# First mixer: twelve sums of squares per layer as two rounded products

## The chip, the cores and the metric

The kernel runs on one core of a Trainium2 chip. The metric is the device time of one execution in microseconds. Five engines work side by side, each with its own queue of instructions in order: TensorE (PE in the profile; its weight loads, PEld, overlap its products), VectorE (DVE), ScalarE (ACT), GpSimd (POOL) and SyncE (SP, which here only starts transfers). They wait for each other by semaphores.

## The reference, cut to what matters

Two stacks of two layers each work on 256 rows of 1024 features. A layer of the first stack is feed-forward, mixer, feed-forward. The change lies in the mixer of the first stack, where the queries and keys of both branches are normalised for each head of 128 features:

```python
def l2norm(x):
    xf = x.astype(jnp.float32)
    return xf * lax.rsqrt(jnp.sum(xf * xf, axis=-1, keepdims=True) + L2_EPS)

def hybrid_mixer(h, w_in, conv_w, ...):
    dn_qkv, dn_z, dn_b, dn_a, sb_q, sb_k, sb_v, gate_a, gate_b = split_cols(h @ w_in)
    qkv = jax.nn.silu(causal_depthwise_conv(dn_qkv, conv_w))
    q, k, v = jnp.split(qkv, 3, axis=-1)
    q = l2norm(to_heads(q, DN_HEADS, DN_HEAD_DIM))
    k = l2norm(to_heads(k, DN_HEADS, DN_HEAD_DIM))
    ...
    o_a = gated_delta_rule_chunked(q, k, v, g, beta)
    ...
    qb = rmsnorm(to_heads(sb_q, SB_HEADS, SB_HEAD_DIM), sb_q_norm)
    kb = rmsnorm(to_heads(sb_k, SB_HEADS, SB_HEAD_DIM), sb_k_norm)
    o_b = stick_breaking_attention(qb, kb, vb)
```

Each of the four (q, k of one branch, sq, sk of the other) has eight heads. Two heads are handled together, so there are sixteen sums of squares in a layer, numbered 0 to 15 here in the order in which they are made.

## The kernel before

The big products are made from weights and inputs that are split in two: a rounded part (`whi`, `xhi`, type float32r) and the rest (`wlo`, `xlo`), and three products of these parts stand for one (`product3`, lines 275 to 277). A weight unit is 128x2048 numbers in one of three slots. For each unit SyncE loads it (`load_unit`, line 246), ScalarE rounds it (`split_hi`, 252), VectorE forms the rest (`split_lo`, 267), and TensorE multiplies.

The first mixer (`mix1_pe`, `mix1_act`, `mix1_dve`, `mix1_pool`, one function for each engine) runs a loop over 28 units of two heads, in the order of the table `IN1`: sk0, sq0, q0, sv0, sk1, q1, sq1, sv1, and so on. The order of work on each engine is what these functions write out; nothing reorders it. `NORM` is the list of the sixteen units that have a norm, `SILU` that of the units which go through a silu, `CONV` that of the units with a convolution. What is done for unit n is spread over the turns of the loop:

- turn n: TensorE multiplies unit n; ScalarE copies it out of its bank (`keep_unit_act`, 880 to 884); VectorE does the convolution (1040, 1044).
- turn n+1: the silu: ScalarE's Abs, Exp, Ln (852 to 856), VectorE's minimum (866), ScalarE's last Exp (861) at the end of its turn, GpSimd's product (`silu_pool`, 871).
- turn n+2: ScalarE squares it into `sqr`, one of two buffers (921).
- turn n+3: TensorE, behind the products of unit n+3, multiplies the squares with a 128x128 matrix of ones (779): the sum over the 128 features, in every row of a bank. It is a product of plain fp32 numbers.
- turn n+4: ScalarE's Ln and Exp of the sum (928, 933); turn n+5: VectorE's scaling (1006, 1008).

Behind the sum, TensorE has in some turns the small products of the stick-breaking attention (1158 to 1182), one head after another, with ScalarE's Abs, Exp, Ln and weights (1199 to 1210), VectorE's parts (1192, 1219, 1224) and the copies of the result to `yhi` and `ylo` (1214, 1228). After the loop comes the delta rule (`mix1_delta_*`).

`yhi` and `ylo` hold the stick-breaking result, head g in column g, and are otherwise free in this loop.

## Time and profile before

| | |
|---|---|
| time, median of 3 runs | 2453.53 us (2451.59 to 2453.79) |
| span of the profiled execution, first to last instruction | 2447.8 us |
| TensorE busy | 2402.2 us, 98% |
| VectorE busy | 1537.0 us, 63% |
| ScalarE busy | 1380.4 us, 56% |
| GpSimd busy | 143.5 us, 6% |
| granted TensorE clock, mean | 0.994 |
| fp32 sums of squares (line 779) | 32 products of 128x512, 64 records |

The span is shorter than the time of an execution by what lies before its first and behind its last instruction; the time of the profiled execution itself is not listed apart from the three runs. The records of TensorE's products are pipelined: a 128x256 product has a record of 0.28 us, but the next one starts 0.12 us after it, so times are read from start to start. Records of the other engines overlap a little too. An fp32 product shows as two records. The loop of the mixer that is changed runs from about 213 to 415 us in layer 0, and from about 988 to 1190 us in layer 1.

### The profile page before, as it was taken

Reading aid. Unit: us, or ns where it says so; the run is one execution under the profiler, and the core shown is the slowest. Engines: PE = TensorE matmul, PEld = TensorE weight load, DVE = VectorE, ACT = ScalarE, POOL = GpSimd, SP = SyncE. Lnnn points to the kernel's source line nnn. Section 1 sums busy time; section 2 is a strip of 40 time slices with the busy share of each in tenths; the row PEclk is TensorE's granted clock in tenths of the full one; section 3 lists DMA queues with packets and bytes.
Section 4 is the critical chain, followed back from the end, with each engine's and each line's share of the span. In section 5 each row is a group of like instructions: output and inputs, shape, how many; then the busy total and the mean of one; then the engine's idle time right before and its main releaser. Section 6 shows DMA issues by size and latency. Waiting matters only on the chain.

```text
span 2447.8 us, 40865 instructions
## 1 busy us (share of the span) xinstructions
PE 2402.2 (98%) x17253; PEld 2238.3 (91%) x17253; DVE 1537.0 (63%) x1867; ACT 1380.4 (56%) x1854; POOL 143.5 (6%) x117
## 2 busy tenths in 40 slices
PE   7999999999999999999999999999999999999998
PEld 7998999998998999899999899888989989888998
DVE  5555678746555655667865655568585455958545
ACT  5455788265555554678635554546654454665444
POOL 0000013000000000001300000000030000004000
PEclk9999999999999999999999999999999999999999
DMA  6554443234554555444314555544445654435553
GB/s 227 194 183 150 160 138 121 87 104 157 201 182 166 190 189 181 148 144 134 119 53 161 175 181 190 191 127 122 137 163 186 200 189 137 130 121 175 192 191 121
DMA packets 312310, 386.58 MB, mean 158 GB/s; under 512 B 10796, under 2 KB 287296, under 8 KB 312128
## 3 DMA queue, kind: packets, MB, share of 16 engines
q1 hardware_dynamic: 311848, 383.87, 47.6%
q8 instruction: 137, 2.24, 0.4%
q14 instruction: 45, 0.37, 0.0%
q10 hardware_dynamic: 280, 0.10, 0.0%
HBM read 382.89 MB, written 1.06 MB: 157 GB/s over the span
## 4 chain that ended last, share of the span: by engine, by line
PE 87%; DVE 7%; ACT 4%; issue 2%; DMA 0%; SPq 0%; DVEq 0%; ACTq 0%
PE bank L275 26%; PE bank L276 25%; PE bank L277 25%; DVE arena L1044 2%; DVE wlo L267 2%; PE bank L1306 1%; PE bank L1311 1%; PE bank L779 1%; ACT whi L252 1%; PE bank L1317 1%; PE bank L1891 1%; PE bank L1283 1%; DVE x L325 1%; DVE arena L2179 1%; ACT arena L356 0%
## 5 line engine op out<-in xcount | busy, mean ns | idle before, releaser
L275 PE MATMUL bank<-xhi,whi 128*128 128x256 f32 x3712 | 1065.9, 287 | 5.6 <-ACT xhi L383 3.5
L276 PE MATMUL bank<-xlo,whi 128*128 128x256 f32 x3712 | 1053.3, 284 | 0.0
L277 PE MATMUL bank<-xhi,wlo 128*128 128x256 f32 x3712 | 1053.3, 284 | 0.0
L267 DVE TENSOR_TENSOR wlo<-raw,whi 128x2048 fp32r<-128x2048 f32 x360 | 831.2, 2312 | 337.8 <-ACT whi L252 334.2
L252 ACT ACTIVATE whi<-raw 128x2048 fp32r<-128x2048 f32 x351 | 669.1, 1907 | 231.4 <-PE bank L277 229.1
L275 PEld LDWEIGHTS bank<-xhi,whi 128*128 128x128 f32 x3712 | 715.1, 193 | 15.3 <-issue 8.3
L276 PEld LDWEIGHTS bank<-xlo,whi 128*128 128x128 f32 x3712 | 715.3, 193 | 4.7 <-issue 1.9
L277 PEld LDWEIGHTS bank<-xhi,wlo 128*128 128x128 f32 x3712 | 714.8, 193 | 0.0
L275 PE MATMUL bank<-whi,yhi 128*128 128x512 f32 x608 | 237.5, 391 | 0.0
L276 PE MATMUL bank<-wlo,yhi 128*128 128x512 f32 x608 | 237.4, 390 | 0.0
L277 PE MATMUL bank<-whi,ylo 128*128 128x512 f32 x608 | 236.5, 389 | 0.0
L277 PEld LDWEIGHTS bank<-whi,ylo 128*128 128x128 f32 x608 | 114.1, 188 | 24.1
L275 PEld LDWEIGHTS bank<-whi,yhi 128*128 128x128 f32 x608 | 114.5, 188 | 22.0
L276 PEld LDWEIGHTS bank<-wlo,yhi 128*128 128x128 f32 x608 | 114.4, 188 | 21.2
L2318 DVE TENSOR_SCALAR arena<-bank 128x512 f32<-128x512 f32 x32 | 22.1, 692 | 148.5 <-PE bank L277 148.5
L606 DVE SCALAR_TENSOR_TENSOR arena<-bank,arena 128x512 f32<-128x512 f32 x44 | 30.4, 692 | 134.4 <-ACT arena L533 134.4
L529 ACT ACTIVATE arena<-bank 128x512 f32<-128x512 f32 x44 | 26.3, 597 | 149.6 <-PE bank L277 149.6
L275 PE MATMUL bank<-yhi,whi 128*128 128x256 f32 x384 | 108.8, 283 | 0.0
L277 PE MATMUL bank<-yhi,wlo 128*128 128x256 f32 x384 | 108.7, 283 | 0.0
L276 PE MATMUL bank<-ylo,whi 128*128 128x256 f32 x384 | 108.7, 283 | 0.0
L871 POOL TENSOR_TENSOR arena<-arena 128x512 f32<-128x512 f32 x32 | 46.1, 1440 | 1058.2 <-ACT arena L861 1058.2
L275 PE MATMUL bank<-whi,xhi 128*128 128x256 f32 (+1 forms) x320 | 105.0, 328 | 0.0
(383 smaller groups left out, 2906.1 us busy)
## 6 DMA issues: line engine op xcount, KB each, us to landing
raw<-in_w_in SPq DMA_DIRECT2D x92, 1024.0 KB, 4.9
raw<-in_ffn_w_in SPq DMA_DIRECT2D x88, 1024.0 KB, 5.1
raw<-in_ffn_w_out SPq DMA_DIRECT2D x44, 1024.0 KB, 4.8
raw<-in_w_gate SPq DMA_DIRECT2D x32, 1024.0 KB, 5.4
raw<-in_w_up SPq DMA_DIRECT2D x32, 1024.0 KB, 5.4
raw<-in_w_down SPq DMA_DIRECT2D x32, 1024.0 KB, 4.9
raw<-in_w_branch_b SPq DMA_DIRECT2D x8, 1024.0 KB, 5.2
raw<-in_w_branch_a SPq DMA_DIRECT2D x8, 1024.0 KB, 5.2
```

The source lines that it names most:

```text
L252: e.activation(whi[s][:], raw[s][:], ACT.Copy).then_inc(hi_done[s], 1)
L267: e.tensor_tensor(wlo[s][:], raw[s][:], whi[s][:].bitcast(F32), ALU.subtract).then_inc(lo_done[s], 1)
L275: e.matmul(o, ahi, bhi, start=start, stop=False, skip_group_check=True)
L276: e.matmul(o, ahi, blo, start=False, stop=False, skip_group_check=True)
L277: return e.matmul(o, alo, bhi, start=False, stop=stop, skip_group_check=True)
L325: return e.scalar_tensor_tensor(part, bank[2 * t + h][:], scale, part, ALU.mult, ALU.add)
L529: e.activation(eg, gate_of(i)[:], ACT.Abs).then_inc(abs_gate, 1)
L606: e.scalar_tensor_tensor(eg, gate_of(i)[:], 0.0, eg, ALU.min, ALU.subtract).then_inc(log_sigmoid, 1)
L779: e.matmul(bank[2 + m % 2][:], ones, sqr[m % 2], start=True, stop=True).then_inc(V["square_sum"].sem, 1)
L871: e.tensor_tensor(home(n), home(n), sg[m % 2], ALU.mult).then_inc(V["silu"].sem, 1)
L1044: ins = e.scalar_tensor_tensor(o, src, w, o, ALU.mult, ALU.add)
L1283: mm = e.matmul(bank[0][:, c * BLK:(c + 1) * BLK], M_blocks[:, :, c], const("row_of"), start=True, stop=True)
```

## The change

For the first twelve of the sixteen sums in each layer (`ROUNDED = 12`), ScalarE squares the input twice, once to fp32 (`sqr`) as before and once to the rounded type (`sqh`, in columns 4 to 7 of `yhi`). GpSimd forms the rest, square minus rounded square, into `sql` (columns 4 to 7 of `ylo`). TensorE multiplies both parts with a rounded matrix of ones (`ones_r`), two products of rounded numbers into the same bank in place of one of fp32 numbers. The matrix is rounded by ScalarE at the start of each mixer. The four last sums stay as they were. The stick-breaking result of head 4 now waits for the twelfth sum, since it goes to the columns that are borrowed.

```diff
+        ones_r = sb("ones_r", [P, P], F32R)
...
+        ROUNDED = 12
...
+        sqh = [yhi[:, 4 + 2 * i:6 + 2 * i, :].rearrange("p c t -> p (c t)") for i in range(2)]
+        sql = [ylo[:, 4 + 2 * i:6 + 2 * i, :].rearrange("p c t -> p (c t)") for i in range(2)]
...
                 if n - 3 in NORM:
                     m = NORM.index(n - 3)
+                    if l == 0 and m == 0:
+                        e.wait_ge(*V["ones_rounded"](l))
                     e.wait_ge(*V["squared"](l, m))
+                    if m < ROUNDED:
+                        e.wait_ge(*V["square_hi"](l, m))
+                        e.wait_ge(*V["square_lo"](l, m))
                     if m >= 2:
                         e.wait_ge(*V["ln_sum"](l, m - 2))
-                    e.matmul(bank[2 + m % 2][:], ones, sqr[m % 2], start=True, stop=True).then_inc(V["square_sum"].sem, 1)
+                    if m < ROUNDED:
+                        e.matmul(bank[2 + m % 2][:], ones_r[:], sqh[m % 2], start=True, stop=False)
+                        mm = e.matmul(bank[2 + m % 2][:], ones_r[:], sql[m % 2], start=False, stop=True)
+                    else:
+                        mm = e.matmul(bank[2 + m % 2][:], ones, sqr[m % 2], start=True, stop=True)
+                    mm.then_inc(V["square_sum"].sem, 1)
...
             e.activation(ba_hi[:], ba_raw[:], ACT.Copy).then_inc(V["ba_hi_done"].sem, 1)
+            e.activation(ones_r[:], ones, ACT.Copy).then_inc(V["ones_rounded"].sem, 1)
...
                     e.activation(sqr[m % 2], home(n - 2), ACT.Square).then_inc(V["squared"].sem, 1)
+                    if m < ROUNDED:
+                        e.activation(sqh[m % 2], home(n - 2), ACT.Square).then_inc(V["square_hi"].sem, 1)
...
             e.wait_ge(*V["o_product"](l, g))
+            if g == 4:
+                e.wait_ge(*V["square_sum"](l, ROUNDED - 1))
             e.activation(yhi[:, g, :], bank[6 + g % 2][:, 0:256], ACT.Copy).then_inc(V["o_hi"].sem, 1)
...
                 if n - 1 in SILU and n < N1:
                     silu_pool(e, l, n - 1)
+                if n - 2 in NORM[:ROUNDED]:
+                    m = NORM.index(n - 2)
+                    e.wait_ge(*V["squared"](l, m))
+                    e.wait_ge(*V["square_hi"](l, m))
+                    finish_waits(e)
+                    e.tensor_tensor(sql[m % 2], sqr[m % 2], sqh[m % 2].bitcast(F32), ALU.subtract)\
+                     .then_inc(V["square_lo"].sem, 1)
```

The numbers at a row's start are lines; those of the changed kernel are larger by the lines put in. On GpSimd, the loop of layer 0 before the change: L871 is the product of the silu.

```order
L2389 AFFINE_SELECT later_keys<-later_keys 128x128 x2
L871 TENSOR_TENSOR arena<-arena 128x512 x15
L1539 TENSOR_TENSOR arena<-arena,table 128x512 x3
```

And after it, with L885 for the silu's product and L1569 for the new subtraction:

```order
L1569 TENSOR_TENSOR ylo<-arena,yhi 128x512
L885 TENSOR_TENSOR arena<-arena 128x512
L1569 TENSOR_TENSOR ylo<-arena,yhi 128x512 x2
L885 TENSOR_TENSOR arena<-arena 128x512
L1569 TENSOR_TENSOR ylo<-arena,yhi 128x512 x3
L885 TENSOR_TENSOR arena<-arena 128x512
L1569 TENSOR_TENSOR ylo<-arena,yhi 128x512 x2
L885 TENSOR_TENSOR arena<-arena 128x512
L1569 TENSOR_TENSOR ylo<-arena,yhi 128x512 x2
L885 TENSOR_TENSOR arena<-arena 128x512
L1569 TENSOR_TENSOR ylo<-arena,yhi 128x512 x2
L885 TENSOR_TENSOR arena<-arena 128x512 x10
```

The twelve subtractions stand between the first five silus; those of sums 1, 3, 8 and 10 come in the same turn as a silu, right behind its product.

On ScalarE, in the turn of sum 8 (unit 10) of layer 0 before the change: copy of unit 12, stick weights, Square, Ln and Exp of the sum two turns back, the last Exp of the silu of unit 11, rounding of the next weights.

```order
L882 ACTIVATE arena<-bank 128x2x256
L1210 ACTIVATE arena<-arena 128x384
L921 ACTIVATE arena<-arena 128x512
L928 ACTIVATE arena<-bank,const_cols 128x512
L933 ACTIVATE arena<-arena,const_cols 128x512
L861 ACTIVATE arena<-arena 128x512
L252 ACTIVATE whi<-raw 128x2048
```

And after it:

```order
L896 ACTIVATE arena<-bank 128x2x256
L1227 ACTIVATE arena<-arena 128x384
L936 ACTIVATE arena<-arena 128x512
L938 ACTIVATE yhi<-arena 128x512
L945 ACTIVATE arena<-bank,const_cols 128x512
L950 ACTIVATE arena<-arena,const_cols 128x512
L875 ACTIVATE arena<-arena 128x512
L253 ACTIVATE whi<-raw 128x2048
```

The second Square (L938) stands between the first and everything else of the turn, the silu's last Exp (now L875) among it.

On TensorE at the same sum, before the change:

```order
L277 MATMUL bank<-xhi,wlo 128x256
L779 MATMUL bank<-arena,table 128x512
L1180 MATMUL bank<-arena 128x256
L1182 MATMUL bank<-arena 128x128
L1158 MATMUL bank<-arena 128x256
```

And after it:

```order
L278 MATMUL bank<-xhi,wlo 128x256
L789 MATMUL bank<-yhi,ones_r 128x512
L790 MATMUL bank<-ylo,ones_r 128x512
L1197 MATMUL bank<-arena 128x256
L1199 MATMUL bank<-arena 128x128
L1175 MATMUL bank<-arena 128x256
```

The sum keeps its place behind the unit's last product and ahead of the stick products, as two instructions in place of one.

## Rows read from the trace of the kernel before

**Rows 1.** Page, costliest groups: count, busy us, mean ns, idle us before them

```profile
L275 PE MATMUL bank<-xhi,whi 128*128 128x256 f32 x3712 | 1065.9, 287 | 5.6 <-ACT xhi L383 3.5
```

**Rows 2.** Stages: us, busy PE PEld DVE ACT POOL (x instructions), PEclk, DMA share, GB/s

```profile
250.00:410.00 160.00, 159.43 (x1224) 150.82 (x1223) 116.40 (x162) 129.32 (x180) 17.07 (x13) 1.00 0.45 147
```

**Rows 3.** Timeline of TensorE at sum 3: start us, length us, engine, line, operation

```profile
263.70 1.02 PE L779 MATMUL bank<-arena,table 128*128 128x512 f32 x2
264.56 0.59 PE L1166 MATMUL bank<-arena,table 128*128 128x256 f32 x2
```

**Rows 4.** Timeline of TensorE in the feed-forward part, rounded products of 128x512

```profile
202.51 0.39 PE L275 MATMUL bank<-whi,yhi 128*128 128x512 f32 x1
202.74 0.39 PE L276 MATMUL bank<-wlo,yhi 128*128 128x512 f32 x1
```

**Rows 5.** Timeline of all engines at sum 0; in brackets idle us and releaser

```profile
236.47 0.61 ACT L921 ACTIVATE arena<-arena 128x512 f32<-128x512 f32 x1
...
237.00 1.90 ACT L252 ACTIVATE whi<-raw 128x2048 fp32r<-128x2048 f32 x1
...
237.14 1.12 PE L779 MATMUL bank<-arena,table 128*128 128x512 f32 x2 [0.25 <-ACT arena L921]
```

**Rows 6.** Timeline of all engines ahead of sum 1

```profile
241.22 0.62 ACT L921 ACTIVATE arena<-arena 128x512 f32<-128x512 f32 x1
...
241.85 0.63 ACT L861 ACTIVATE arena<-arena 128x512 f32<-128x512 f32 x1
...
242.67 1.30 POOL L871 TENSOR_TENSOR arena<-arena 128x512 f32<-128x512 f32 x1 [239.12 <-ACT arena L861]
...
243.99 1.10 PE L779 MATMUL bank<-arena,table 128*128 128x512 f32 x2
```

**Rows 7.** Timeline of GpSimd ahead of sum 3, of ScalarE and TensorE at sum 4

```profile
260.54 1.30 POOL L871 TENSOR_TENSOR arena<-arena 128x512 f32<-128x512 f32 x1 [16.58 <-ACT arena L861]
...
267.14 0.61 ACT L921 ACTIVATE arena<-arena 128x512 f32<-128x512 f32 x1
...
271.19 1.02 PE L779 MATMUL bank<-arena,table 128*128 128x512 f32 x2
```

**Rows 8.** Timeline of all engines ahead of sum 8

```profile
302.80 0.53 ACT L1210 ACTIVATE arena<-arena 128x384 f32<-128x384 f32 x1 [1.33 <-DVE arena L1224]
...
305.09 0.62 ACT L861 ACTIVATE arena<-arena 128x512 f32<-128x512 f32 x1
...
305.78 1.30 POOL L871 TENSOR_TENSOR arena<-arena 128x512 f32<-128x512 f32 x1 [19.99 <-ACT arena L861]
...
307.54 2.29 DVE L267 TENSOR_TENSOR wlo<-raw,whi 128x2048 fp32r<-128x2048 f32 x1 [1.63 <-ACT whi L252]
...
307.77 1.02 PE L779 MATMUL bank<-arena,table 128*128 128x512 f32 x2
```

**Rows 9.** Timelines of VectorE and GpSimd: alone, side by side, and two in a row

```profile
231.81 0.62 DVE L1040 TENSOR_SCALAR arena<-pre,conv_w 128x256 f32<-128x256 f32 x2 [2.08 <-ACT pre L880]
...
363.31 1.65 DVE L1040 TENSOR_SCALAR arena<-pre,conv_w 128x256 f32<-128x256 f32 x2
...
363.48 1.33 POOL L871 TENSOR_TENSOR arena<-arena 128x512 f32<-128x512 f32 x1 [4.20 <-ACT arena L861]
...
421.68 2.51 POOL L1553 TENSOR_TENSOR arena<-arena,table 128x512 f32<-128x512 f32 x2
...
431.69 2.28 DVE L267 TENSOR_TENSOR wlo<-raw,whi 128x2048 fp32r<-128x2048 f32 x1
431.90 3.19 POOL L871 TENSOR_TENSOR arena<-arena 128x512 f32<-128x512 f32 x1 [3.49 <-ACT arena L861]
```

**Rows 10.** Timeline of GpSimd and TensorE ahead of sum 10

```profile
326.77 1.30 POOL L871 TENSOR_TENSOR arena<-arena 128x512 f32<-128x512 f32 x1 [19.68 <-ACT arena L861]
...
330.25 1.02 PE L779 MATMUL bank<-arena,table 128*128 128x512 f32 x2
```

**Rows 11.** Table of stages, a part of the delta rule (columns as in rows 2)

```profile
433.00:443.00 10.00, 10.00 (x47) 10.00 (x48) 5.12 (x21) 2.18 (x2) 4.87 (x5) 0.51 0.52 177
```

More of the change, by code:

```diff
@@ L691, in hybrid_stack_kernel @@
             pre_copied=12, tap=48, kept=16, s_abs=16, s_exp=16, s_ln=16, s_min=16, s_sigmoid=16, silu=16,
-            squared=16, square_sum=16, ln_sum=16, rnorm=16, normed=16,
+            squared=16, square_hi=ROUNDED, square_lo=ROUNDED, ones_rounded=1, square_sum=16, ln_sum=16, rnorm=16, normed=16,
             z_product=8, z_kept=8, z_abs=8, z_exp=8, z_ln=8, softplus=8, r_product=8, z_minus=8,
```

## The prediction

> **What bounds the kernel now.** I read the page's busy shares and its costliest groups first. TensorE is the engine to watch: the largest group is the weight product in rounded parts, 1065.9 us busy in that line alone, with 5.6 us of idle time ahead of it in the whole program [rows 1]. The table of stages says the same of the place that is changed: from 250 to 410 us, the loop over the 28 units in layer 0, TensorE's records cover 159.43 of 160 us at the full clock [rows 2]. So in this loop every time that TensorE saves is a gain, and every wait that it gets is a loss of the same size; the other engines matter only where TensorE waits for them. Next I read the timeline at single sums, on all engines, to see how long TensorE takes for one and who is ready how long before it. Layer 1 shows the same pattern 774.6 us later, so I work out one layer and double it.
>
> **What a sum costs and will cost.** One fp32 product of 128x512 stands as two matmul records. The sum at 263.70 us is followed by the next product at 264.56 us: 0.86 us of TensorE [rows 3]. The 128x512 products of rounded operands in the feed-forward part start 0.225 us apart [rows 4]. The new form is two of these into one bank, 0.45 us. The saving is 0.41 us for each sum, with the same number of weight loads. Twelve sums give 4.9 us a layer, 9.8 us in all. Bounds: if the two rounded products cost as much as the fp32 records, 0 us; better than 0.23 us each is shown by no row. I take the row of the same operand form, 0.225 us. This would be the result if nothing else were late.
>
> **What it adds.** ScalarE gets a second Square for each of the twelve. A Square lasts 0.61 us, but the next instruction starts 0.53 us after it [rows 5], so each adds 0.52 us to what ScalarE does later in the same turn of the loop. GpSimd gets a subtraction 128x512. Its nearest row is the multiplication of the same shape, 1.30 us, and two in a row take 2.51 us, 1.25 us apart [rows 6, 9]. GpSimd starts 0.07 to 0.18 us after ScalarE's record ends (305.71 to 305.78 and 242.48 to 242.67) [rows 6, 8]; TensorE started 0.06 us after the Square it waited for [rows 5]. So from the end of a Square to the start of its sum there were 0.06 us at least, and now there are 0.52 + 0.1 + 1.30 + 0.05 = 1.97 us at least. In between, GpSimd's queue is in order: in the turn in which unit n+1 has a silu, the subtraction for unit n stands behind that silu's multiplication, which waits for ScalarE's last exponential of the turn. That is so at sums 1, 3, 8 and 10. The ones matrix is rounded by one ScalarE copy ahead of the layer's norm, where ScalarE then waits for the residual; it costs nothing. The wait at the fifth stick head for sum 11 is met two turns earlier and costs nothing.
>
> **Sum by sum, as lateness against the old trace.** I follow by how much TensorE starts each sum later than before; after it the 0.41 us is taken off.
> - Sum 0: the Square ran from 236.47 to 237.08 and TensorE, already idle for 0.25 us, began at 237.14 [rows 5]. Now: 237.08 + 0.52 + 0.15 + 1.30 + 0.05 = 239.10 us. Late by 1.96, after it 1.55 us. This is sure to be paid, since the wait was already there.
> - Sum 1: its Square moves from 241.22 by 0.52 us; the silu exponential of unit 2 (line 861) was at 241.85 and waited for VectorE's minimum, and now stands behind the second Square, at 242.78 us. The multiplication that was at 242.67 us comes at 243.55, the subtraction 1.25 us later at 244.80, its end at 246.10, the sum at 246.15 us in place of 243.99 [rows 6]. Late by 2.16, after it 1.75 us: TensorE waits another 0.6 us here.
> - Sums 2 to 7: the shortest time from the end of a Square to its sum is at sum 4, 267.75 to 271.19 us [rows 7], and 1.97 us are wanted, behind a ScalarE that is 0.52 us late. Only sum 3 has a silu in front: its multiplication began at 260.54 us [rows 7], now 261.06; the subtraction follows 1.25 us later and ends at 263.61, and the sum was at 263.70 us [rows 3]: just enough. No wait; six savings of 0.41 take the lateness from 1.75 to 0.11 us at sum 5 and -0.71 us after sum 7.
> - Sum 8: ScalarE's chain before it starts with the stick weights at 302.80 us, which wait for VectorE (line 1224), and runs without a gap to the exponential at 305.09, the multiplication at 305.78, and the sum at 307.77 us [rows 8]. VectorE in turn is held up by the subtraction of sum 7 (below) by about 0.6 us, which leaves its line 1224 at the old place, 0.07 us later, although TensorE comes 0.82 us earlier by the savings of sums 6 and 7. So: 305.09 + 0.07 + 0.52 = 305.68; multiplication 306.37; subtraction 307.62 to 308.92; sum 308.97 us, plus the 0.11 us that the layer was late at sum 5. Late by 1.31, after it 0.90 us. The wait of 2.0 us eats the savings of sums 6 and 7 as well. Were VectorE not held up, it would be 0.6 us less.
> - Sums 9 to 11: sum 10 has a silu in front, whose multiplication began at 326.77 us [rows 10]; 0.52 + 1.25 + 1.30 + 0.06 us later is 329.90 us, against 330.25. No wait, by 0.35 us. Three more savings: 0.90 - 1.23 = -0.33 us at the layer's end.
> A layer gets 0.33 us shorter, both 0.7 us. By parts: 4.9 us saved a layer, 4.6 us more waiting (1.96, 0.6 and 2.0 us at three sums). The profiled span of 2447.8 us becomes 2447.1 us; the median of the runs is 2453.53 us, 5.7 us above that span for what lies around it, so the forecast is 2452.9 us.
>
> **VectorE and GpSimd hold each other up.** In the trace they take turns. The two-input multiplication that began at 431.90 us, 0.2 us behind a VectorE subtraction of 2.28 us, lasted 3.19 in place of 1.30 us: to the end of VectorE's and then its own. The other way round, a pair of tensor-scalar operations at 363.31 us took 1.65 in place of 0.62 us because a GpSimd multiplication ran from 363.48 to 364.81 us [rows 9]. The Trainium skill, page GPSIMD Engine Reference, section Key points, says that GpSimd shares its SBUF interfaces with VectorE and contends with VectorE instructions in a 2-port mode or with two SBUF inputs. The trace agrees and adds that whoever has begun finishes first; by the page alone, which gives no size, nothing in the sum would change. For this change it makes each new subtraction a possible delay of 1 us for VectorE, which does not matter where VectorE has time, and makes the order at sums 1 and 8 matter: the subtraction begins 1.94 us after the exponential (0.69 + 1.25), and VectorE's 2.29 us subtraction behind ScalarE's rounding copy begins 2.45 us after it (307.54 - 305.09) [rows 8]. GpSimd wins by 0.5 us.
>
> **The rivals.**
> - Everything is hidden: the waits that I placed at sums 0, 1 and 8 do not come, and 9.8 us are gained, 2443.7 us. Against it stands sum 0, where TensorE waited for the Square itself.
> - The turn at the memory is lost: slower. If VectorE's rounding rest gets in front of the subtraction at sums 1 and 8, each pays the rest of 2.29 us less the head start, some 2.1 us more. From a GpSimd start 0.5 us later than I took, this is what happens. Four times 2.1 us: 2461.3 us. For it: one case in the trace in which GpSimd came second [rows 9]. Against it: the margin of 0.5 us is several times the spread of 0.07 to 0.18 us of GpSimd's start.
> - GpSimd's handover is 0.3 us slower than I took, without losing its turn: three sums pay 0.3 us more, and sums 3, 4, 10 and 11, which I found to have 0.1 to 0.5 us to spare, begin to pay 0.1 to 0.2 us. Some 1.6 us a layer, 2456.1 us: within my bound for no change.
> - TensorE's clock falls to its lower level, 1.2 GHz, after the wait of about 2.3 us at sum 0. In the delta part the granted clock was 0.51 from 433 to 443 us, which at half speed costs 5 us [rows 11]. Such a drop in both layers gives about 2463 us. Against it: sum 0 comes out of a dense stretch and goes into one.
> - The change does not do what it says: the rounded products of this form run as slowly as the fp32 ones. Then nothing is saved, and the waits stay: 2462.7 us.
>
> **How the numbers follow.** The forecast with its own range of 2450 to 2456 us gets 0.60, the slower handover 0.16, the lost turn 0.08, the clock 0.04, no faster products 0.02, all hidden 0.04; 0.06 is left for waits that are smaller than mine by half or more (2.3 us a layer less, 2448.3 us). What a measurement of this kernel can tell from no change is about 0.2%, 4.9 us: faster means under 2448.6 us, slower over 2458.4 us. Faster: 0.04 + 0.06, 0.10. Slower: 0.08 + 0.04 + 0.02 and a little of the slow handover, 0.16. The rest, 0.74, is no change. The range goes down to 2449.0 us and up to 2458.0 us.
>
> **What would show it.** In the changed profile, right if: the two new products start about 0.23 us apart and the pair takes 0.45 us; TensorE's idle time ahead of the sums is 2.2 to 2.4 us at sum 0, about 0.6 us at sum 1 and 2 us at sum 8, put down to GpSimd, and near 0 elsewhere; ScalarE's second Square lasts 0.6 us; the GpSimd subtraction is 1.3 us where it runs alone; VectorE's conv operations beside it grow by up to 1 us. Wrong if sums 3, 10 or 11 wait too, if a subtraction at sum 1 or 8 lasts over 2 us, if the granted clock falls in 236 to 410 us, or if TensorE waits somewhere else in the loop because VectorE or ScalarE became late (the stick sums of line 1166 behind sum 3 are the nearest, with under 0.2 us to spare).

## The result and the profile after

| | before | after |
|---|---|---|
| time, median of 8 runs each | 2453.82 us (2451.59 to 2454.29) | 2459.25 us (2457.99 to 2461.06) |
| ratio, 95% interval | | 1.0027 (1.0017 to 1.0037) |
| span of the profiled execution | 2447.8 us | 2456.2 us |
| granted TensorE clock, mean | 0.994 | 0.990 |
| GpSimd busy | 143.5 us | 178.0 us |

The changed kernel is 0.27% slower, some 6 us. That is above the range that I gave, which ended at 2458.0 us. TensorE's own large group is as it was; the page has these lines for it now, the second of which answers to [rows 1]:

```profile
PE 2402.3 (98%) x17253; PEld 2246.4 (91%) x17253; DVE 1547.4 (63%) x1867; ACT 1391.9 (57%) x1880; POOL 178.0 (7%) x141
...
L276 PE MATMUL bank<-xhi,whi 128*128 128x256 f32 x3712 | 1064.7, 287 | 5.2 <-ACT xhi L384 3.2
```

**The saving.** The timeline of TensorE at sum 5 of the changed kernel (start us, length us, engine, line, operation), to be held against [rows 3]:

```profile
279.37 0.39 PE L789 MATMUL bank<-yhi,ones_r 128*128 128x512 f32 x1
279.60 0.40 PE L790 MATMUL bank<-ylo,ones_r 128*128 128x512 f32 x1
279.83 0.59 PE L1183 MATMUL bank<-arena,table 128*128 128x256 f32 x2
```

The two rounded products start 0.23 us apart and the stick product follows 0.46 us after the first, where the fp32 sum took 0.86 us. The saving of 0.40 us is there at every sum that TensorE doesn't wait for.

**The waits.** The timeline of ScalarE, GpSimd and TensorE at sum 0 (in brackets the idle time before, in us, and what ended it), for [rows 5]:

```profile
235.91 0.61 ACT L936 ACTIVATE arena<-arena 128x512 f32<-128x512 f32 x1
...
236.43 0.61 ACT L938 ACTIVATE yhi<-arena 128x512 fp32r<-128x512 f32 x1
...
237.34 1.27 POOL L1569 TENSOR_TENSOR ylo<-arena,yhi 128x512 fp32r<-128x512 f32 x1 [233.79 <-ACT yhi L938]
...
238.75 0.47 PE L789 MATMUL bank<-yhi,ones_r 128*128 128x512 f32 x1 [2.42 <-POOL ylo L1569]
239.07 0.40 PE L790 MATMUL bank<-ylo,ones_r 128*128 128x512 f32 x1
```

The same at sum 1, for [rows 6]:

```profile
242.21 0.62 ACT L875 ACTIVATE arena<-arena 128x512 f32<-128x512 f32 x1
...
242.91 1.30 POOL L885 TENSOR_TENSOR arena<-arena 128x512 f32<-128x512 f32 x1 [4.30 <-ACT arena L875]
...
244.16 1.29 POOL L1569 TENSOR_TENSOR ylo<-arena,yhi 128x512 fp32r<-128x512 f32 x1
...
244.66 2.93 DVE L268 TENSOR_TENSOR wlo<-raw,whi 128x2048 fp32r<-128x2048 f32 x1 [2.89 <-ACT whi L253]
...
245.59 0.47 PE L789 MATMUL bank<-yhi,ones_r 128*128 128x512 f32 x1 [0.25 <-POOL ylo L1569]
```

And at sum 8, for [rows 8]:

```profile
305.68 0.61 ACT L875 ACTIVATE arena<-arena 128x512 f32<-128x512 f32 x1
...
306.38 1.28 POOL L885 TENSOR_TENSOR arena<-arena 128x512 f32<-128x512 f32 x1 [10.05 <-ACT arena L875]
...
307.61 1.27 POOL L1569 TENSOR_TENSOR ylo<-arena,yhi 128x512 fp32r<-128x512 f32 x1
...
309.14 0.47 PE L789 MATMUL bank<-yhi,ones_r 128*128 128x512 f32 x1 [2.16 <-ACT arena L936]
```

TensorE waits 2.42 us at sum 0, 0.25 us at sum 1 and 2.16 us at sum 8. The last bracket names a ScalarE Square (line 936), but it is GpSimd's subtraction that ends at 308.88 us, 0.26 us ahead of the sum; a wait for three semaphores is put down to whatever the profile shows last, and the next Square, of another sum, happens to lie there. In layer 1 the waits are 2.30, 0 and 2.16 us. At no other sum of the two loops does TensorE wait longer than 0.03 us. GpSimd won its turn at the memory at sums 1 and 8 as forecast: at sum 1 it is VectorE's subtraction behind it that grows, to 2.93 us.

**What the prediction didn't have.** Stretches of the timeline of the changed kernel (us, busy PE, PEld, DVE, ACT, POOL with counts, granted clock of TensorE, share of the DMA engines, GB/s); the first line answers to [rows 2]:

```profile
250.00:410.00 160.00, 157.18 (x1220) 151.93 (x1219) 120.53 (x159) 132.10 (x191) 30.11 (x22) 0.99 0.47 146
...
238.90:242.30 3.40, 3.40 (x28) 3.31 (x29) 2.87 (x2) 3.33 (x7) 0.00 (x0) 1.00 0.02 5
309.80:313.20 3.40, 3.40 (x15) 3.06 (x14) 2.11 (x3) 1.32 (x3) 2.35 (x1) 0.51 0.24 48
1016.40:1019.80 3.40, 3.04 (x12) 2.88 (x13) 2.79 (x2) 3.33 (x6) 0.22 (x1) 0.50 0.00 0
1088.10:1091.50 3.40, 3.40 (x10) 2.86 (x11) 1.89 (x1) 1.68 (x3) 2.37 (x1) 0.50 0.12 15
```

And of the kernel before, the loop of layer 0 and the places of the last three lines:

```profile
213.00:415.00 202.00, 201.18 (x1558) 191.21 (x1558) 142.06 (x192) 153.18 (x218) 19.00 (x15) 1.00 0.45 147
...
309.80:313.20 3.40, 3.40 (x31) 3.40 (x30) 1.81 (x4) 2.94 (x5) 0.00 (x0) 1.00 0.64 207
...
1016.40:1019.80 3.40, 3.40 (x26) 2.92 (x25) 0.90 (x2) 3.39 (x5) 1.31 (x1) 1.00 0.83 271
1088.10:1091.50 3.40, 3.40 (x24) 2.89 (x23) 2.58 (x2) 1.65 (x3) 0.00 (x0) 1.00 0.23 76
```

Read the column of the clock. In the changed kernel TensorE is busy for all of 309.8 to 313.2 us, but at 0.51, its lower level of 1.2 GHz: it starts 15 products in the time in which it starts 28 at the full clock (238.9 to 242.3 us). The kernel before had no such stretch in either loop; the changed one has three. One begins 0.7 us behind the end of a long wait, the other two in the last 0.4 us of one. Half speed for 3.4 us would be 1.7 us of work in a dense stream. Measured it is a little less: from sum 8 to sum 9 TensorE takes 9.21 and 9.22 us in the two layers here, and 7.61 us in layer 0 of the kernel without sum 0 (below), where the same wait was followed by the full clock. That is 1.6 us. Behind the wait at sum 0 of layer 1 the net cost is 0.8 us, since TensorE then no longer waits at sum 1; in layer 0 the clock stayed up there.

The profile shows one execution of each kernel, but the mean granted clock is on record for all of them. It is 0.989 or 0.990 in all eight executions of the changed kernel, and 0.992 to 0.994 in 51 of the 52 executions of the kernel before that were timed beside the experiments (0.991 in the other one). So the changed kernel spends more time at the lower clock in every execution.

The 8.4 us between the two spans, by the lateness of TensorE against the trace of before (the share of the clock is an estimate from the 1.6 and 0.8 us above, outside the loops from 3.4 us at half speed):

| part | change, us | of it half-speed clock |
|---|---|---|
| up to the wait at sum 0 of layer 0 | -0.6 | not taken apart |
| loop, layer 0 | +2.0 | 1.6 |
| delta rule and feed-forward up to layer 1's loop | +1.5 | 1.5 to 1.7 (one stretch, at 422.5 us) |
| loop, layer 1 | +2.9 | 2.4 (two stretches, 0.8 and 1.6) |
| delta rule of layer 1 | +1.1 | none more than before; not taken apart |
| second stack | +1.5 | 1.5 to 1.7 (one stretch more, at 2142.8 us) |

Without the clock the two loops would have cost some 0.9 us together; I had forecast a gain of 0.7 us. The two rows outside the loops with a stretch more are not shown to be the work of the change. The kernel before has the same wait of 2 us in its delta rule, and the profiles of all the other twelve kernels have a stretch where the changed one has it in the second stack: there it is the one profile of before that is the exception.

### The profile page after: what moved, and what is told of

Read it like the earlier page. It is cut to its first block, busy times and chain, and to the rows that moved or that the text cites. A ratio compares the mean times of both kernels' runs of the same rounds, so it can differ in the third digit from the quotient of the medians.

```text
span 2456.2 us, 40966 instructions
## 1 busy us (share of the span) xinstructions
PE 2402.3 (98%) x17253; PEld 2246.4 (91%) x17253; DVE 1547.4 (63%) x1867; ACT 1391.9 (57%) x1880; POOL 178.0 (7%) x141
## 4 chain that ended last, share of the span: by engine, by line
PE 82%; DVE 9%; ACT 6%; issue 3%; DMA 0%; POOL 0%; SPq 0%; DVEq 0%; ACTq 0%; POOLq 0%
PE bank L276 24%; PE bank L277 24%; PE bank L278 24%; DVE arena L1061 3%; DVE wlo L268 2%; ACT whi L253 2%; PE bank L1325 1%; PE bank L1330 1%; DVE arena L1057 1%; PE bank L1917 1%; PE bank L1336 1%; PE bank L1302 1%; DVE x L326 1%; DVE arena L2205 1%; ACT arena L357 0%
## 5 line engine op out<-in xcount | busy, mean ns | idle before, releaser
L277 PE MATMUL bank<-wlo,xhi 128*128 128x256 f32 (+1 forms) x320 | 104.1, 325 | 0.0
```

Source lines behind the costliest of these rows:

```text
L277: e.matmul(o, ahi, blo, start=False, stop=False, skip_group_check=True)
```

## Experiments

The theories at the start were these. First, the sum by waits holds, and what is missing is the lower clock behind the waits. Second, in its place, a spread cost: GpSimd's 24 subtractions slow VectorE everywhere and with it the stream (called C in some of the expectations), or the 24 second Squares make ScalarE late (called B). A spread cost would stay if the waits were taken away.

| kernel | time, us | before on the same chip, us | ratio, 95% interval |
|---|---|---|---|
| e1_no_gpsimd | 2445.91 | 2452.03 | 0.9971 (0.9959 to 0.9982) |
| e2_waits_only | 2461.44 | 2452.03 | 1.0039 (1.0026 to 1.0053) |
| e3_swapped | 2451.70 | 2452.03 | 0.9996 (0.9987 to 1.0005) |
| e4_swapped_from_sum_1 | 2444.45 | 2452.03 | 0.9970 (0.9959 to 0.9981) |
| e5_without_0_1_8 | 2450.01 | 2453.67 | 0.9985 (0.9976 to 0.9993) |
| e6_without_0 | 2454.37 | 2453.67 | 1.0009 (1.0000 to 1.0018) |
| e7_without_8 | 2453.81 | 2453.67 | 1.0001 (0.9992 to 1.0010) |
| e8_swapped_1_to_10 | 2445.55 | 2453.67 | 0.9973 (0.9962 to 0.9984) |
| w1_waits_short | 2465.47 | 2454.95 | 1.0052 (1.0029 to 1.0075) |
| w2_waits_middle | 2470.72 | 2454.95 | 1.0068 (1.0045 to 1.0091) |
| w3_waits_long | 2479.13 | 2454.95 | 1.0107 (1.0072 to 1.0141) |
| w4_waits_longest | 2492.93 | 2454.95 | 1.0163 (1.0128 to 1.0198) |

Most rows are medians of five to eleven executions; w1 and w2 have three, w3 and w4 two.

### Without GpSimd

Both products read the rounded square, and the subtraction and its waits are gone:

```diff
-                        e.wait_ge(*V["square_lo"](l, m))
...
-                        mm = e.matmul(bank[2 + m % 2][:], ones_r[:], sql[m % 2], start=False, stop=True)
+                        mm = e.matmul(bank[2 + m % 2][:], ones_r[:], sqh[m % 2], start=False, stop=True)
...
-                    e.tensor_tensor(sql[m % 2], sqr[m % 2], sqh[m % 2].bitcast(F32), ALU.subtract)\
-                     .then_inc(V["square_lo"].sem, 1)
```

> Both Squares and two rounded products for the twelve sums, but without the GpSimd subtraction and without a wait for it: the second product reads the rounded square again, so the sum is of the wrong numbers. Theory A (TensorE's waits for GpSimd, and half-speed stretches of its clock set off by them): all of the saving comes through, 24 x 0.41 = 9.8 us, less 0.5 us at sum 0 of each layer for the second Square: about 2445 us, 9 us under the kernel before, no wait over 1 us at a sum, and no half-speed stretch in the loops. Theory B (the added work on ScalarE delays the rest of the loop): 2452 us or more.

Measured: 2445.91 us, 6 us under the kernel before on the same chip where 9 were expected. In the profile its two loops are 8.4 us shorter than before, so nearly all of the saving is there, and no stretch at half speed lies in them; what takes the rest back lies outside the loops and wasn't taken apart. TensorE's wait at sum 0 is 0.86 us, for the second Square alone, and there is none at sums 1 and 8:

```profile
238.31 0.47 PE L788 MATMUL bank<-yhi,ones_r 128*128 128x512 f32 x1 [0.86 <-ACT yhi L937]
238.62 0.40 PE L789 MATMUL bank<-yhi,ones_r 128*128 128x512 f32 x1
```

All 24 second Squares are still in this kernel, and it is faster than before. After sum 0 TensorE gains 0.39 to 0.42 us at each rounded sum. So ScalarE's extra work has no spread cost of note; what costs comes with GpSimd. This run alone doesn't say whether by its place in the chain ahead of a sum or by its turns at the memory.

### The waits without the saving

All of the change stays, but the product is the fp32 one of `sqr`; the rounded square and its rest are made and not read:

```diff
-                    if m < ROUNDED:
-                        e.matmul(bank[2 + m % 2][:], ones_r[:], sqh[m % 2], start=True, stop=False)
-                        mm = e.matmul(bank[2 + m % 2][:], ones_r[:], sql[m % 2], start=False, stop=True)
-                    else:
-                        mm = e.matmul(bank[2 + m % 2][:], ones, sqr[m % 2], start=True, stop=True)
+                    mm = e.matmul(bank[2 + m % 2][:], ones, sqr[m % 2], start=True, stop=True)
```

> All waits, Squares and subtractions of the change, but the sums are fp32 products of the unrounded squares as before. Theory A: the changed kernel without its saving, 9 to 11 us above it, 2469 us; the sums start as late as in the changed kernel plus 0.41 us for each one before, except sum 8, where the chain that it waits for is not moved by 0.8 us of it. Rival (the rounded products of two operands cost more than 0.45 us, so that there was no saving to lose): within 3 us of the changed kernel.

Measured: 2461.44 us, only 2 to 3 us above the changed kernel, although 24 savings of 0.40 us, 9.6 us, are gone. The expectation was a miss by some 8 us, and the time is the one that its rival gave, "within 3 us of the changed kernel". But the rival's reason, rounded products that save nothing, is ruled out by the trace of the changed kernel, where the pair takes 0.46 us in place of 0.86. TensorE at sums 0 and 8:

```profile
238.99 1.10 PE L788 MATMUL bank<-arena,table 128*128 128x512 f32 x2 [2.43 <-POOL ylo L1565]
...
311.45 1.10 PE L788 MATMUL bank<-arena,table 128*128 128x512 f32 x2 [1.47 <-ACT arena L932]
```

Without the savings TensorE reaches sum 8 later and waits 1.47 us there in place of 2.16, and it doesn't wait at sum 1. What the savings of sums 6 and 7 give is taken back by the wait at sum 8, in the changed kernel as in my sum. The other part is the clock. In the profiled execution of this kernel, the shortest of its five (2458.12 us; the longest took 2464.13), no stretch at half speed lies in the loops:

```profile
239.10:242.50 3.40, 3.40 (x24) 2.92 (x25) 2.89 (x2) 3.33 (x7) 0.00 (x0) 1.00 0.02 5
311.50:314.90 3.40, 3.40 (x21) 2.82 (x22) 2.85 (x3) 2.03 (x4) 2.40 (x1) 1.00 0.10 17
1017.30:1020.70 3.40, 3.40 (x24) 2.92 (x25) 2.90 (x2) 3.34 (x7) 0.00 (x0) 1.00 0.00 0
1089.90:1093.30 3.40, 3.40 (x21) 2.82 (x22) 2.85 (x3) 2.04 (x4) 2.40 (x1) 1.00 0.10 19
```

Its loops are each 4.1 us longer than before: 2.2 us at sum 0, 1.6 us at sum 8, the rest at sums 3 and 4. That is the waits alone, 8.2 us in both layers. The changed kernel without the clock's part lost some 0.9 us there, so the saving brings some 7.3 us, and the clock takes 4.0 of them back. The two profiled spans come out alike, 2456.3 and 2456.2 us, for different reasons. Only one execution was profiled, but the mean granted clock of all five is on record: 0.995 in the two shortest (2458.12 and 2460.15 us), 0.993 in the next (2461.44 us), 0.992 in the two longest (2463.73 and 2464.13 us). So the longer executions of this kernel had more of the lower clock, though not shown where.

### GpSimd's two instructions in the other order

The subtraction is written ahead of the silu product, so it no longer stands behind the last exponential of ScalarE's turn:

```diff
-                if n - 1 in SILU and n < N1:
-                    silu_pool(e, l, n - 1)
                 if n - 2 in NORM[:ROUNDED]:
...
+                if n - 1 in SILU and n < N1:
+                    silu_pool(e, l, n - 1)
```

> The changed kernel with GpSimd's two operations of a turn swapped: the subtraction of unit n stands ahead of the silu's product of unit n+1. Theory A: the waits at sums 1 and 8 (0.6 and 2.1 us) and the half-speed stretches behind sum 8 go, the wait at sum 0 of 2.3 us stays: a layer is 4.9 - 2.0 = 2.9 us shorter than before, less 0 to 1.7 us for a half-speed stretch behind sum 0: 2448 to 2451.5 us. Theory C (what costs is that GpSimd and VectorE hold each other up, 12 x 1 us a layer): the subtractions are still there, 2455 us or more.

Measured: 2451.70 us, at the upper end of the 2448 to 2451.5 us of theory A and under the 2455 of theory C; the same as before within 0.1%, and 7 to 8 us better than the changed kernel. GpSimd at sum 1, and TensorE at sum 0:

```profile
239.32 0.76 PE L789 MATMUL bank<-yhi,ones_r 128*128 128x512 f32 x1 [2.43 <-POOL ylo L1567]
...
243.03 1.30 POOL L1567 TENSOR_TENSOR ylo<-arena,yhi 128x512 fp32r<-128x512 f32 x1 [3.86 <-ACT yhi L938]
244.29 1.30 POOL L885 TENSOR_TENSOR arena<-arena 128x512 f32<-128x512 f32 x1
```

The waits at sums 1 and 8 are gone; that at sum 0 stays, and in both layers it is followed by the lower clock:

```profile
239.20:242.50 3.30, 3.18 (x13) 3.02 (x14) 2.89 (x2) 3.24 (x7) 0.00 (x0) 0.50 0.03 5
1014.00:1017.40 3.40, 3.40 (x16) 3.21 (x16) 2.89 (x2) 3.33 (x8) 0.00 (x0) 0.50 0.00 0
```

The record of one product in it, 0.76 us, is near twice the 0.47 us that it has behind the same wait at the full clock. A small new wait of 0.67 to 0.69 us stands at sum 11.

### The other order, and sum 0 left as it was

As above, and `ROUNDED` is a list of sums (the counters go by the place in the list):

```diff
-        ROUNDED = 12
+        ROUNDED = (1, 2, 3, 4, 5, 6, 7, 8, 9, 10, 11)
```

> As the swapped kernel, and sum 0 of each layer is left an fp32 product of one Square: eleven rounded sums. Theory A: no wait beyond those of the kernel before, 22 x 0.41 = 9.0 us less than before: 2444.8 us, half-speed stretches only where the kernel before has them. Theory C: the contention remains, 2453 us or more.

Measured: 2444.45 us, 0.30% faster than before. TensorE at sums 0 and 11:

```profile
238.30 1.12 PE L792 MATMUL bank<-arena,table 128*128 128x512 f32 x2 [0.24 <-ACT arena L936]
...
336.06 0.47 PE L789 MATMUL bank<-yhi,ones_r 128*128 128x512 f32 x1 [0.69 <-POOL ylo L1567]
```

The wait at sum 0 is back to the 0.24 us that it always was; no stretch at half speed lies in either loop (one begins behind the delta rule's wait, at 419 us). From sum 1 to sum 10 TensorE gains 0.3 to 0.4 us at each. The kernel holds 22 second Squares and 22 subtractions, so both forms of a spread cost fall: GpSimd's turns still fall between VectorE's instructions, and TensorE gains at these sums all the same.

### Single sums left out, in the order of the change

Three kernels keep GpSimd's order and leave some sums as fp32 products:

```diff
-        ROUNDED = 12
+        ROUNDED = (1, 2, 3, 4, 5, 6, 7, 8, 9, 10, 11)
...
-        ROUNDED = 12
+        ROUNDED = (0, 1, 2, 3, 4, 5, 6, 7, 9, 10, 11)
...
-        ROUNDED = 12
+        ROUNDED = (1, 2, 3, 4, 5, 6, 7, 9, 10, 11)
```

> The changed kernel with sum 0 left as an fp32 product. Theory A: the wait at sum 0 goes (1.96 us a layer), one saving goes too (0.41), but sum 1 now waits about 1.6 us in place of 0.3, since TensorE comes earlier: lateness after sum 1 of 1.2 in place of 1.75 us; that and the half-speed stretch behind sum 0 gone (some 1.7 us in half of the layers): 2.5 to 3.5 us less than the changed kernel, with the wait at sum 8 and its half-speed stretches as they are. About 2455 us.

> The changed kernel with sum 8 left as an fp32 product. Theory A: the wait of 2.2 us at sum 8 goes, less one saving of 0.41 us, and the half-speed stretch behind it, which the changed kernel's trace shows in both layers: 2 x (1.8 + up to 1.7) = 3.6 to 7 us less than the changed kernel: 2451 to 2454.5 us. With waits alone (no part of the clock) it would be 3.6 us.

> The changed kernel in its own order on GpSimd, but sums 0, 1 and 8 left as fp32 products of one Square: nine rounded sums. Theory A: none of the long waits is left; 18 x 0.41 = 7.4 us less than the kernel before, 2444.6 us beside 2452; half-speed stretches only where the kernel before has them. Rival (the contention of GpSimd with VectorE costs by itself): 2449 us or more.

The last expectation, like the kernel's label, speaks of sums 0, 1 and 8 and of nine rounded sums a layer. The kernel that ran left out sums 0 and 8 only: sum 1 was still rounded, ten in all. What it would give without sum 1 wasn't tried. Its time, 2450.01 us, misses the 2444.6 us of theory A and lies where the rival, a cost of the contention by itself, had put it (2449 us or more). The waits account for most of that: at sum 1 TensorE waits 1.56 and 1.47 us in the two layers. The best kernel below rounds ten sums a layer as well and has no such wait; its loops gain 3.6 us more by the profiles, 3.0 of them these two waits. The rival would have to cost that kernel as much.

Measured against the ratio of the changed kernel: 4.4 us less without sum 0 and 6.4 us less without sum 8; against the kernel before, the first is 0.1% slower or the same and the second is the same. The first was expected at 2.5 to 3.5 us and gave somewhat more, the second at 3.6 to 7 us; each difference of two ratios is uncertain by some 3 us, so they agree with the theory more than they measure it. Without sums 0 and 8 together the kernel is 0.15% faster than before. Leaving out sum 0 moves a part of its wait to sum 1, here in the kernel without sums 0 and 8 (a subtraction late behind the silu product, a TensorE that arrives early):

```profile
243.26 1.29 POOL L885 TENSOR_TENSOR arena<-arena 128x512 f32<-128x512 f32 x1 [239.72 <-ACT arena L875]
244.52 1.26 POOL L1569 TENSOR_TENSOR ylo<-arena,yhi 128x512 fp32r<-128x512 f32 x1
245.92 0.47 PE L789 MATMUL bank<-yhi,ones_r 128*128 128x512 f32 x1 [1.56 <-ACT arena L936]
```

So the order on GpSimd is worth more than the choice of sums. The kernels without one sum also show that the same wait can be followed by either clock. Without sum 0, behind the two waits of 2.17 us at sum 8 of the two layers:

```profile
310.10:313.50 3.40, 3.40 (x24) 3.21 (x25) 3.24 (x3) 2.41 (x5) 2.39 (x1) 1.00 0.12 13
1087.50:1090.90 3.40, 3.40 (x16) 3.29 (x15) 1.71 (x3) 1.98 (x5) 1.62 (x1) 0.51 0.45 122
```

Without sum 8, behind the waits of 2.43 and 2.30 us at sum 0:

```profile
239.90:243.30 3.40, 3.40 (x16) 3.24 (x15) 2.74 (x2) 3.34 (x7) 0.00 (x0) 0.50 0.06 9
1015.30:1018.70 3.40, 3.40 (x27) 3.31 (x28) 2.90 (x2) 3.34 (x7) 0.00 (x0) 1.00 0.00 0
```

### Waits of four lengths put into the kernel before

To measure the clock by itself, the kernel before gets five waits a layer: behind sums 2, 4, 6, 8 and 10 TensorE waits for GpSimd to clear free columns of `yhi` and `ylo`, which begins when the sum ends. The computation is untouched. The first clears 1024 numbers a partition; the second 512 more, the third 1024 more, the fourth another 768 behind a semaphore:

```diff
+                    if m in HELD:
+                        e.wait_ge(*V["held"](l, HELD.index(m)))
...
+                    e.wait_ge(*V["square_sum"](l, m))
+                    up = e.memset(free[0][:, 0:1024], 0.0)
+                    up = e.memset(free[1][:, 0:1024], 0.0)
+                    up.then_inc(V["held"].sem, 1)
```

(The third is shown; the first has one clearing of 1024, the second 1024 and 512.)

> The kernel before with ten added waits of TensorE, behind sums 2, 4, 6, 8 and 10 of each layer: each until GpSimd has cleared 128x1024 free numbers once the sum is done, about 1.3 us of idle time. Theory A (a wait of TensorE over about 2 us sets off a half-speed stretch of its clock in most cases, which costs 1.7 us on top): none here, 10 x 1.3: 2465 us. Theory B (the clock has nothing to do with waits of this length): the same 2465 us.

> The same with 128x1536 numbers, about 1.8 us of idle time each. Theory A: few half-speed stretches or none, 2470 to 2475 us. Theory B: 2470 us.

> The same with 128x2048 numbers, about 2.3 us each, the length of the waits at sums 0 and 8 of the changed kernel. Theory A: a half-speed stretch behind five to eight of the ten waits, 10 x 2.3 + 6 x 1.7: 2485 us, and those stretches stand in the table of stages right behind the waits. Theory B: none behind them, 2475 us.

> The same with 128x2816 numbers in three parts, about 3.1 us each. Theory A: a half-speed stretch behind nearly all of the ten, 10 x 3.1 + 9 x 1.7: 2498 us. Theory B: 2483 us.

Measured: 2465.47, 2470.72, 2479.13 and 2492.93 us. The first two are as expected by both theories. The other two lie between theory A (2485 and 2498 us) and theory B (2475 and 2483 us). The waits came out shorter than the 1.3, 1.8, 2.3 and 3.1 us that I had expected, which is 3 us in each of these two sums. TensorE behind sum 4 with the shortest, the long and the longest wait:

```profile
274.22 0.70 PE L1184 MATMUL bank<-arena 128*128 128x256 f32 x2 [1.07 <-POOL yhi L1550]
```

```profile
276.94 0.70 PE L1184 MATMUL bank<-arena 128*128 128x256 f32 x2 [1.96 <-POOL ylo L1551]
```

```profile
281.51 0.88 PE L1184 MATMUL bank<-arena 128*128 128x256 f32 x2 [2.75 <-POOL yhi L1554]
```

And the 3.4 us behind this wait, with the shortest, the middle, the long and the longest:

```profile
274.20:277.60 3.40, 3.38 (x25) 3.27 (x26) 1.73 (x5) 1.59 (x4) 0.00 (x0) 1.00 0.92 281
```

```profile
276.50:279.90 3.40, 3.40 (x27) 3.30 (x27) 1.99 (x6) 1.41 (x3) 0.00 (x0) 1.00 0.89 300
```

```profile
277.70:281.10 3.40, 3.40 (x17) 3.22 (x16) 1.90 (x5) 1.28 (x3) 0.00 (x0) 0.51 0.62 212
```

```profile
281.90:285.30 3.40, 3.40 (x15) 3.13 (x14) 1.13 (x4) 0.54 (x2) 0.00 (x0) 0.50 0.47 164
```

| kernel | length of its ten waits, us | waits followed by the lower clock | span, us | above w1, both loops: TensorE's lateness / its waits |
|---|---|---|---|---|
| w1 | 1.07 to 1.10 | 0 | 2463.6 | |
| w2 | 1.53 to 1.71 | 0 | 2468.9 | 4.9 / 4.9 |
| w3 | 1.96 to 2.14 | 3 | 2479.8 | 13.8 / 9.2 |
| w4 | 2.75 to 2.94 | 8 | 2493.5 | 30.5 / 17.1 |

Up to the middle length the loops grow by what TensorE waits. Beyond it they grow by 4.6 and 13.4 us more than the waits do, with three and eight of them followed by the lower clock. Single waits show the price: in w3 a wait of 1.96 us makes TensorE 2.2 us late where the clock stays up and 3.7 to 3.8 where it falls; in w4 a wait of 2.75 us makes 3.0 and 4.5 to 4.6. So a fall costs 1.5 to 1.6 us, and any of these waits 0.27 us beyond its idle time. The counts behind theory A in the last two expectations were too high: three falls in w3 where five to eight were expected, eight in w4 where it was nearly all ten.

In all profiles together, the waits of TensorE in the two loops that were followed by the lower clock are: none of 26 between 1.07 and 1.71 us, 3 of 10 between 1.96 and 2.14, 3 of 4 at 2.16 to 2.17, 4 of 8 at 2.30 to 2.43, 8 of 10 at 2.75 to 2.94. Outside the loops, the wait of 2.03 to 2.08 us in the delta rule, which all fourteen kernels have in both layers, was followed by it in 14 of 28 cases. And in one place of the feed-forward part a wait of 1.52 us with a second one of 0.41 us right behind it was followed by it in 4 of the 14 profiles, so a wait under 1.7 us isn't safe where another one is near. These are counts of this program's waits, not a rule of when the clock falls, and one profile for each kernel is little for the middle of it.

### The best of both

GpSimd's order swapped, and neither sum 0 nor sum 11, whose small wait is new in that order:

```diff
-        ROUNDED = 12
+        ROUNDED = (1, 2, 3, 4, 5, 6, 7, 8, 9, 10)
```

> The swapped kernel with sums 1 to 10 rounded only: sum 11 in the swapped kernel has a wait of 0.7 us that eats its saving. Ten savings of 0.41 us a layer, no wait beyond those of the kernel before: 8.2 us less than it and 0.5 us less than the swapped kernel from sum 1: 2443.8 us. By theory A this is the fastest of all versions here.

Measured: 2445.55 us, 0.27% faster than before, where 2443.8 us and the fastest version of all were expected. TensorE waits 0.25 us at sum 0, as it did, and at no other sum; sum 11 has no bracket:

```profile
334.18 1.02 PE L792 MATMUL bank<-arena,table 128*128 128x512 f32 x2
```

The wait of 0.69 us at sum 11 is gone, and with it that sum's saving of 0.40 us. Behind sum 15 TensorE waits 0.59 us for VectorE's part of the stick-breaking attention, 0.27 us more than before. This kernel and the one with eleven sums can't be told apart; both beat the kernel before by some 7 us and the changed one by some 13 to 14.

## Why the prediction was wrong

**The saving was right.** 0.41 us for each sum was forecast from [rows 3, 4], 0.40 was measured. The first product behind a wait costs 0.08 us more (0.31 us to the next one in place of 0.23), three times a layer.

**The waits were right in place and near in size.** Forecast 2.2 to 2.4, 0.6 and 2.0 us at sums 0, 1 and 8; measured 2.42, 0.25 and 2.16 in layer 0. To compare times, note that the changed kernel's profile runs 0.56 us ahead of the old one before sum 0, so its lateness is taken from there. At sum 0 it is 2.17 us (forecast 1.96): the handover was under-sized, ScalarE to GpSimd 0.30 us (237.04 to 237.34) where I had 0.15, and GpSimd to TensorE 0.14 us where I had 0.05. At sum 1 it is 2.16 us, as forecast, since that chain runs apart from TensorE; the wait is smaller than forecast only because TensorE arrives later. After six more savings it is 0.01 us at sum 7 (forecast -0.30). At sum 8 it is 1.93 us (forecast 1.31): ScalarE's exponential was 0.45 us later than I had it, 0.3 of which is TensorE's own lateness at sum 5, and the last handover took 0.26 us in place of 0.05. By the layer's end this makes 0.4 us late without the clock, where I had 0.33 us early. My rival of a slower handover was so partly true: 0.7 us a layer of the 1.6 that it gave, and no wait at sums 3, 10 or 11.

**VectorE and GpSimd took their turns as read from [rows 9].** A subtraction lasts 1.27 to 1.30 us alone and up to 2.37 behind VectorE (sum 9, harmless); at sums 1 and 8 it came first. The Trainium skill, page GPSIMD Engine Reference, section Key points, has the contention but no size; the trace agrees with it, and the size stayed off TensorE's path.

**The step that failed is the clock.** I gave the fall to 1.2 GHz a chance of 0.04, for sum 0 alone, "Against it: sum 0 comes out of a dense stretch and goes into one", and the sum has it at nothing. That reason was wrong: in the loops of all profiles a wait of some two microseconds or more in the middle of a dense stream was followed by the lower clock in 18 of 32 cases. It was also too narrow, since the wait at sum 8 that I had worked out, 2.0 us, is of the same kind. And its price, 5 us, was taken from a stage of another kind [rows 11]: there the clock is low for 10 us on end, from 433.1 us, and no wait of TensorE stands within the 12 us ahead of it. Behind the waits of the loop a fall costs 1.5 to 1.6 us, or 0.8 where it hides a wait at sum 1. Two or three such falls in the four long waits, as the counts above have it, are some 3.2 to 4.8 us; with 1.5 us for the handover in both layers, my sum of 2452.9 us becomes some 2457.6 to 2459.2 us, and 2459.25 were measured. The agreement is not to be read too closely: in the profile of the changed kernel there are two stretches more outside the loops, one behind a wait of 2.06 us in the delta rule of layer 0 that the kernel before has as well (2.05 us), one in the second stack, where the program didn't change. Neither is shown to come from the change, and which of the four long waits have a fall in the other seven executions isn't known.

The Trainium skill, page TensorE: Matmul & The Clock Gate, section "HAM oscillation — how this bites in real kernels", tells of a kernel whose waits for data bring the lower clock back, so that the work behind each wait pays a second time. The trace agrees in kind, with waits of 2.16 us that cost 1.6 us more; the waits in that page's example are longer than these. The profile of before could not have settled the matter: its two waits of 2.05 us, in the delta rule of both layers, were followed by no fall within the next 10 us, while the same two waits were followed by one in half of the cases over all profiles.

**A point of bookkeeping.** I took 5.7 us for what lies around the profiled span. It is 1.8 us in every run whose span is known (2457.99 and 2456.2 us after; 2447.42 and 2445.6 us in the swapped kernel without sum 0). The profiled execution of before was simply one of its shortest, about 2449.6 us; over all chips its executions reach from 2449.0 to 2455.3 us. The forecast went by differences, so this didn't move it, but it makes a single pair of spans a poor measure of 0.2%: 8.4 us between the spans, 5.4 between the medians.

## What to carry to other kernels

In this kernel a single wait of TensorE in a dense stream is to be priced by its length, and from some 2 us on with another 1.5 to 1.6 us times the chance that the clock falls; so a link taken out of the chain ahead of such a wait can be worth more than its own length. Where a new step is put between two engines that were just in time, look first at what it stands behind in its own queue: here swapping two instructions on GpSimd and leaving out the one sum without slack turned a loss of 6 us into a gain of 7.

## What the runs showed of the hardware

- In the loops the granted clock of TensorE fell to 0.50 or 0.51 at waits of 1.96 to 2.94 us in 18 of 32 cases, and in none of 26 waits of 1.07 to 1.71 us. The fall came between 0.7 us ahead of the wait's end and 1.4 us behind it, and lasted 3.4 us, once 6.8 us (w4, from 254.6 us). The same wait in two layers of one execution can have either outcome (2.30 and 2.43 us; 2.17 us twice). What decides between them, these runs don't show.
- Such a fall cost TensorE 1.5 to 1.6 us (w3, w4, and the way from sum 8 to sum 9).
- The clock can be low without a wait ahead of it: in the kernel before it was so from 433.1 to 443.4 us, in the delta rule, with TensorE's records covering all of 423 to 453 us.
- A GpSimd subtraction of 128x512 has 1.27 to 1.30 us; its start comes 0.07 to 0.30 us after ScalarE's record ends where GpSimd is idle, and TensorE's start 0.14 to 0.26 us after GpSimd's.
- A clearing of 128x1024 on GpSimd has 0.95 us, against 1.3 us for a subtraction of half the size with two inputs.
